# Reading the 256 moving columns of the stationary-weight products in even, then odd, pieces of 16

## The reference

```python
# first block, layer i
hn = _rmsnorm(h, norm_g[i])
u = hn @ w_in[i]                                  # 2048 x 5632
...                                               # convolution and attention branches
h = h + jnp.concatenate([ya, yb], axis=-1) @ w_out[i]
e = _rmsnorm(p[i] @ w_pe[i], pe_g[i])
h = h + e * jax.nn.sigmoid(h @ w_pg[i])
# second block, layer i
p = h @ (fox_w_in[j] if i % N_MIXERS == 0 else swa_w_in[j])
...                                               # attention
x = x + (y * jax.nn.silu(gate)) @ w_out
```

## Time and profile before

| | |
|---|---|
| median of three executions | 1781.31 us (1780.55 to 1784.65) |
| profiled execution, whole time | 1774.15 us |
| its span, first to last instruction | 1772.4 us |
| TensorE busy | 1755.0 us, 99% |
| VectorE busy | 1309.2 us, 74% |
| ScalarE busy | 901.2 us, 51% |
| DMA, share of 16 engines | 58.6%, 184 GB/s |

### The profile page before, as it was taken

The page is one execution under the profiler, slowest core; times in us unless marked ns, Lnnn a source line. Parts: engine busy times, 40 slices in busy tenths (PEclk is TensorE's granted clock), DMA queues, the critical chain, the costliest instruction groups (busy, mean ns, idle before and its releaser), DMA issues.

```text
span 1772.4 us, 35680 instructions
## 1 busy us (share of the span) xinstructions
PE 1755.0 (99%) x14349; PEld 1686.9 (95%) x14349; DVE 1309.2 (74%) x2085; ACT 901.2 (51%) x1326; POOL 38.5 (2%) x48
## 2 busy tenths in 40 slices
PE   8999999999999999999999999999999999999997
PEld 8999999999999999999999899999989999999886
DVE  7899899977679987998777765656565556667754
ACT  5433665555533465456565463545455453665553
POOL 0000000000000000000000110100100000000000
PEclk9999999999999999999999999999999999999999
DMA  7666555555666664555566665665655556555563
GB/s 233 190 206 194 191 147 176 197 184 195 197 186 205 195 202 143 158 196 193 180 200 184 206 202 179 190 189 180 193 160 167 191 179 187 162 158 171 169 194 131
DMA packets 200082, 326.07 MB, mean 184 GB/s; under 512 B 14911, under 2 KB 66319, under 8 KB 199821
## 3 DMA queue, kind: packets, MB, share of 16 engines
q1 hardware_dynamic: 197085, 320.58, 57.9%
q10 hardware_dynamic: 2864, 3.62, 0.7%
HBM read 320.42 MB, written 2.69 MB: 182 GB/s over the span
## 4 chain that ended last, share of the span: by engine, by line
PE 92%; DVE 5%; DMA 1%; issue 1%; ACT 1%; ACTq 0%; DVEq 0%; POOLq 0%; SPq 0%; POOL 0%
PE g L499 73%; PE g L510 11%; DVE w_lo L898 2%; PE att L600 2%; PE att L645 2%; PE att L624 2%; DVE cacc L1144 2%; PE att L499 1%; ACT w_hi L1533 0%; DMA turned<-q 0%; PE att L789 0%; DMA stage<-in_w_in_dram 0%; DVE glu L1116 0%; PE att L858 0%; PE att L576 0%
## 5 line engine op out<-in xcount | busy, mean ns | idle before, releaser
L898 DVE TENSOR_TENSOR w_lo<-stage,w_hi 128x1024 fp32r<-128x1024 f32 x577 | 706.4, 1232 | 378.4 <-ACT w_hi L1533 377.4
L1533 ACT CAST w_hi<-stage 128x1024 fp32r<-128x1024 f32 x577 | 599.8, 1050 | 618.5 <-PE g L499 403.8
L499 PE MATMUL g<-a_hi,w_hi 128*128 128x256 f32 x2496 | 705.5, 283 | 1.6 <-DVE a_lo L1078 0.9
L499 PE MATMUL g<-a_lo,w_hi 128*128 128x256 f32 x2496 | 696.6, 279 | 0.0
L499 PE MATMUL g<-a_hi,w_lo 128*128 128x256 f32 x2496 | 696.5, 279 | 0.0
L499 PEld LDWEIGHTS g<-a_hi,w_hi 128*128 128x128 f32 x2496 | 469.9, 188 | 12.1 <-issue 8.4
L499 PEld LDWEIGHTS g<-a_lo,w_hi 128*128 128x128 f32 x2496 | 473.1, 190 | 0.0
L499 PEld LDWEIGHTS g<-a_hi,w_lo 128*128 128x128 f32 x2496 | 470.5, 189 | 0.5 <-issue 0.2
L499 PE MATMUL g<-b_hi,w_hi 128*128 128x256 f32 x1440 | 404.5, 281 | 0.1
L499 PE MATMUL g<-b_lo,w_hi 128*128 128x256 f32 x1440 | 401.5, 279 | 0.0
L499 PE MATMUL g<-b_hi,w_lo 128*128 128x256 f32 x1440 | 401.4, 279 | 0.0
(11 more groups left out here) (232 smaller groups left out, 1359.9 us busy)
## 6 DMA issues: line engine op xcount, KB each, us to landing
stage<-in_fox_w_in_dram SPq DMA_DIRECT2D x128, 512.0 KB, 3.7
stage<-in_w_in_dram SPq DMA_DIRECT2D x112, 512.0 KB, 3.8
stage<-in_swa_w_in_dram SPq DMA_DIRECT2D x72, 512.0 KB, 3.9
stage<-in_w_in_dram SPq DMA_DIRECT2D x128, 256.0 KB, 3.1
stage<-in_w_out_dram SPq DMA_DIRECT2D x64, 512.0 KB, 4.2
stage<-in_w_pg_dram SPq DMA_DIRECT2D x64, 512.0 KB, 4.1
stage<-in_fox_w_out_dram SPq DMA_DIRECT2D x32, 512.0 KB, 4.2
stage<-in_swa_w_out_dram SPq DMA_DIRECT2D x32, 512.0 KB, 4.0
```

The source lines that it names most:

```text
L499: mm = pe.matmul(acc[:, j * S:(j + 1) * S], w[:, slot, c0 + j * P:c0 + (j + 1) * P], xx[:, k, :], start=st and m == 0 and j % 2 == 0, stop ...
L898: dve.tensor_tensor(w_lo[:, slot, :], stage[:, slot, :], w_hi[:, slot, :].bitcast(F32), ALU.subtract).then_inc(*t.inc("w_split"))
L1533: act.copy(w_hi[:, slot, :], stage[:, slot, :]).then_inc(*t.inc("w_rounded"))
```

## The change

On line 499 the output and the moving operand go through a new function, `by_sides`. It cuts 256 columns into 16 pieces of 16 columns (64 bytes each in a partition) and orders them as pieces 0, 2, 4, ... 14, then 1, 3, 5, ... 15. As the output is reordered the same way, each number lands where it did before, with the same sum in the same order. No instruction, wait, transfer or buffer is added or taken away. Line 510, line 789 and all others stay.

```diff
+SIDE = 16
...
+def by_sides(ap):
+
+    return ap.rearrange("p (c side e) -> p side c e", side=2, e=SIDE)
...
-                                mm = pe.matmul(acc[:, j * S:(j + 1) * S], w[:, slot, c0 + j * P:c0 + (j + 1) * P],
-                                               xx[:, k, :], start=st and m == 0 and j % 2 == 0, stop=end and m == 2,
+                                mm = pe.matmul(by_sides(acc[:, j * S:(j + 1) * S]), w[:, slot, c0 + j * P:c0 + (j + 1) * P],
+                                               by_sides(xx[:, k, :]), start=st and m == 0 and j % 2 == 0, stop=end and m == 2,
                                                skip_group_check=True)
```

## The result

The changed kernel takes 1834.44 us (median of four, 1833.35 to 1835.46) against 1780.93 us for the kernel before (median of four, 1774.47 to 1784.65): ratio 1.0321, 95% interval 1.030 to 1.0341. It is 53.5 us slower, where the forecast was no change.

What follows compares the result with a forecast made beforehand. TensorE was taken as the bound: number of instructions times distance between starts. Three parts at 0 summed to 12000 x 0 = 0, so 1781.3 us, forecast's own range 1778 to 1785, full range 1740 to 1872.

Steps and rivals of the forecast that it cites:

- the first part of the sum: Line 499's address jumps at input and output: taken to cost nothing, 0; from above 1387 us.
- rival 2: Line 499: every address jump costs one cycle, 80 us (1861 us), or two, 160 us (1941 us); chance 0.19.
- The second part: Line 499: moving and weight pieces meet at equal parity; halfway 116.7 ns against today's 116.2, taken as 0.
- The test that I named: Line 499's distance between starts: one level near 116.7 ns everywhere, `pe` included, would show the second part.
- The third part: Line 499's output: PSUM reads and writes follow each other over the same columns; taken as 0.
- Rival 1: Line 499: piece parities collide more often, 5 to 45 us slower, middle 25 us, 1806 us; chance 0.17.
- Rival 3: Line 499: the upper level goes, all products at 113.35 ns; 35 us less, 1747 us; chance 0.17.
- Rival 4: Line 499: the lost cycle is that of changing sides; 87 us less, 1694 us; chance 0.10.

Runs made afterwards that it cites:

- e4: Kernel before with the unused buffer of 256 numbers in place of 240, so `a` and `b` tiles begin at the weights' parity: 1814.7 us, ratio 1.0197.
- e10: Kernel of product streams alone, 16-column pieces at steps of 0 to 192 columns, plain runs beginning 0 to 128 columns into a tile: 113.3 to 122.2 ns.
- e7: Changed kernel with the unused buffer of 256 numbers in place of 240: 1819.46 us, ratio to the kernel before 1.0238.
- e2: Changed kernel with the even-odd order on the moving operand alone, output in plain order: 1834.52 us, ratio to the kernel before 1.0311.
- e12: Full kernel with even-odd order only on the first product of the next two tiles after other work interrupts the products: 1761.13 us, ratio 0.9905.

## Why the prediction was wrong, point by point

What bounds the kernel was right: TensorE's distance between starts, with nothing hiding a change of it. 12000 x 5.2 ns is the whole loss, other engines did not move, and the products of 512 columns kept their distance. Reading the loss from distances of starts and not from the length of records was needed: a record grew from 283 to 288 ns, 2%, a distance from 113.4 to 121.3, 7%, and from 118.3 to 121.8, 3%.

The step that failed is the first part of the sum, the breaks, put at 0: "I take the lower end: ... while it goes from one 64-byte piece to the next, which it goes on doing as often". It cost 5.2 ns a product, 61.9 us on the line, and all of it at the input (1.0311 for the input alone, 1.0005 for the output). As often is true and jumps are free, as the steps of 80 and 144 showed. But it matters which piece comes next: of four places in turn the even-odd order uses two at a time. The prediction also miscounts the breaks: they are 14 jumps over a piece and one back, 15 in all and not 16, which takes rival 2's cycle a piece from 80 to 75 us. The row at which I could have stopped was there. The loss grew with the columns, and the stream had no spare rate; I used this against the forecast (rival 2) and not in it.

The second part failed in size. The parity of the tiles against the weights does set the level, as the `pe` rows hinted; e4 confirmed it in both directions. My step from there, "about half of the weight pieces would meet it" and so 116.7 ns, has no support: with 32 weight columns, a quarter of the weight pieces, the order costs as much. Nor is it parity alone, but the place among four (e10). The place costs 35 us by itself (e4), the order 54, and both together 39 (e7). The test that I named, one level near 116.7 everywhere, came out as one level at 121.3.

The third part, the output at 0, was right.

Rival 1 had the sign and, at its dear end, most of the size: 12000 products at 120.0 give 45 us, and they came to 121.3. `pe`, which was to tell it from rival 2, did not: it stayed at 120.0 in one stretch and rose to 122.3 in the other, and in e2 in both. But its mechanism, meeting the weight pieces, does not carry the loss, since 32 weight columns lose as much from the order as 128. Rival 2 priced a cycle per piece at 80 us. From 113.3 to 120.0 with 32 weight columns is that cycle to the digit, but its mechanism in general, a cost of a jump, is out; what it named in its second half, pieces of one side that cannot be served in turn, is near to R. The price was too high because more than half of the products stood at the upper level already: from 113.4 to 121.3 is 8 ns, from 118.3 to 121.8 is 3.5. Weighting them as the prediction did, (4973 x 8 + 7027 x 3.5) = 64 us, near the 61.9 measured.

Rival 3, the upper level goes, did not happen with the change but can be had: in e12 the upper level is nearly gone (384 products at 114.1 ns), for 19 us by the medians, where rival 3 had 35. Rival 4 is out: no form with 256 columns went under 113.3 ns in the streams.

The forecast's own time was therefore wrong by 53 us, with the measured one inside the range that rival 2 had stretched to 1872.

## What to carry to other kernels

If TensorE is the bound and its distance between starts is a few per cent above columns divided by clock, look at which addresses it streams, not only at how many: here the same reads in another order cost 3%, another start of a tile 2% (and both together 2.4%, not their sum), and one product in a different order behind each interruption gained 1%. An order that jumps is not dear as such; test a step that jumps but keeps the turn of the places beside one that does not, since only the pair tells the two apart. And when two levels of one instruction appear in a trace of identical work, count which share stands at each before pricing an edit: the gain or loss starts from that mix.

## What the runs showed of the hardware

- The order in which the moving operand of float32r products (256 columns) is read sets their distance. For pieces of 64 bytes at a constant step it repeats after 256 bytes, as if there were four places: with 32 weight columns 113.3 to 116.6 ns when the four are read forwards in turn, 117.8 backwards, 120.0 when two are read, 122.2 when one is; with 128 weight columns 113.3 or 117.8, 117.8, 120.0 to 121.3 and 120.0. Orders with other turns do not all fit (117.8 for one place at a time in quarters, 120.0 for exchanged neighbours with 128 weight columns).
- The output in even-odd order costs nothing with 128 weight columns (117.8 ns as in order; 1.0005 for the kernel).
- The place of the moving tile against the weights counts: with 128 weight columns a plain run takes 113.3 to 120.0 ns depending on where the tile starts modulo 64 columns, and moving the weights changes it too. With 32 weight columns plain runs stood between 113.3 and 120.0.
- For the `a` tiles of this kernel and 128 weight columns the distance of plain products settles at one of two values, 113.3 or 117.8 ns, when a stream starts, and stays there for a thousand products (1068 at 113.4 in one execution, at 117.8 in another). A single other product can move it. What sets it at a start is open: the number of small products ahead went with it in one stream kernel and not in others.
- Float32r products with 128 weight columns do not go below 111.4 to 111.6 ns for 128 to 224 columns; with 32 weight columns 128 columns take 60.0 ns. Products of 512 columns lose 4.7 ns by the even-odd order (233.5 to 238.2).
- Weight columns that lie 16 or 32 elements apart nearly double the distance of plain products, 223.1 and 225.8 ns.
- The even-odd order takes 121.3 ns with 128 weight columns from the kernel's start of the tiles, but 120.0 from an even start or with the odd pieces first. Why is open.
